# Scores of the latent attention heads as three f16 products of scaled high and low parts, in place of f32 products

## What is computed

```python
h = rms_norm(x, g_norm) * (1 + scale[:, None, :]) + shift[:, None, :]
proj = h @ w_in      # split: q_lat, kv_lat, k_rope, z_a, q_b, k_b, v_b, z_b
qa = (rms_norm(q_lat, g_qa) @ w_uq)    # 8 heads of 96, the last 32 rotated
kv = (rms_norm(kv_lat, g_kva) @ w_ukv) # k_nope (64) and va (64) of each head
ka = concat(k_nope, rotate(k_rope))    # the rotary part is shared by the heads
oa = softmax(qa @ ka.T * MLA_SCALE) @ va
ob = softmax(qb @ kb.T * GQA_SCALE) @ vb
x = x + gate * (concat(oa * silu(z_a), ob * silu(z_b)) @ w_out)
```

## Time and profile before

| | |
|---|---|
| median of 3 runs | 2541.19 us (2537.12 to 2541.44) |
| the profiled execution | 2537.28 us, its span 2535.5 us |
| PE busy | 2341.6 us, 92% of the span |
| DVE busy | 1371.3 us, 54% |
| ACT busy | 974.1 us, 38% |
| POOL busy | 790.5 us, 31% |
| mean granted TensorE clock | 0.977 |
| HBM traffic | 128.07 MB, 51 GB/s over the span |

### The profile page before, as it was taken

How to read it: one execution, slowest core, us unless ns; L and a number is a source line. 1 busy time by engine, 2 the same in 40 slices (tenths; PEclk the granted TensorE clock), 3 DMA queues, 4 the chain that set the end, 5 groups by cost and what they waited for, 6 DMA issues and landing times.

```text
span 2535.5 us, 44397 instructions
## 1 busy us (share of the span) xinstructions
PE 2341.6 (92%) x16106; PEld 1392.5 (55%) x16106; DVE 1371.3 (54%) x2444; ACT 974.1 (38%) x2202; POOL 790.5 (31%) x1325
## 2 busy tenths in 40 slices
PE   3888998899999999999989899889999999999997
PEld 1445544456556656656545455445556666665654
DVE  3645454566555555556535444446566555555563
ACT  0233333225444444444422333422354444444442
POOL 0553221664222122123036432146533113212210
PEclk7999999999999999999999999999999999999999
DMA  8712112120000000000412000132000000000001
GB/s 285 253 42 67 50 67 86 50 100 10 18 17 8 25 17 18 16 17 17 165 59 92 18 26 8 42 110 108 9 11 25 17 33 25 8 33 25 0 26 42
DMA packets 63236, 129.43 MB, mean 51 GB/s; under 512 B 6690, under 2 KB 31368, under 8 KB 63132
## 3 DMA queue, kind: packets, MB, share of 16 engines
q1 hardware_dynamic: 63136, 128.09, 14.5%
HBM read 115.44 MB, written 12.63 MB: 51 GB/s over the span
## 4 chain that ended last, share of the span: by engine, by line
PE 72%; DVE 16%; issue 5%; ACT 2%; POOL 2%; DMA 2%; SPq 1%; DVEq 0%; POOLq 0%; ACTq 0%
PE psum L600 55%; PE psum L590 10%; PE psum L808 6%; DVE region L1071 3%; DVE nmax L1054 3%; DVE hT L910 3%; ACT region L1225 1%; POOL region L1279 1%; DVE region L1029 1%; DVE KTa L872 1%; DMA Wout<-in_w_ada 1%; DVE region L1080 1%; PE psum L610 1%; PE psum L594 0%; DVE region L1031 0%
## 5 line engine op out<-in xcount | busy, mean ns | idle before, releaser
L1225 ACT ACTIVATE region<-psum 128x512 f16<-128x512 f32 x640 | 353.5, 594 | 758.5 <-PE psum L590 758.3
L600 PE MATMUL psum<-Wq,hT 128*128 128x512 f32 (+1 forms) x1536 | 611.1, 544 | 6.6 <-DVE KTa L872 5.0
L1071 DVE TENSOR_TENSOR region<-psum,region 128x512 f16<-128x512 f32 x640 | 415.7, 683 | 293.4 <-ACT region L1225 292.7
L590 PE MATMUL psum<-ident,region 128*128 128x128 f32 (+1 forms) x3208 | 436.9, 277 | 25.6 <-DVE Va L966 10.5
L600 PEld LDWEIGHTS psum<-Wq,hT 128*128 128x128 f32 x1536 | 285.0, 191 | 251.2 <-issue 224.9
L1054 DVE TENSOR_REDUCE nmax<-psum 128x1 f32<-128x1024 f32 (+1 forms) x384 | 398.7, 1038 | 40.0 <-PE psum L600 39.0
L590 PEld LDWEIGHTS psum<-ident,region 128*128 128x128 f32 (+1 forms) x3208 | 356.4, 140 | 109.7 <-issue 78.4
L600 PE MATMUL psum<-Wout,region 128*128 128x512 f32 x768 | 354.3, 606 | 9.2 <-DVE region L1039 6.8
L600 PE MATMUL psum<-KTa,region 96*128 96x512 f32 x640 | 312.9, 604 | 18.6 <-DVE region L1029 12.9
L1279 POOL TENSOR_TENSOR region<-region,rope_sb 128x64 f32<-128x64 f32 (+3 forms) x384 | 158.3, 434 | 332.5 <-DVE region L1025 316.1
L1217 ACT ACTIVATE region<-psum,nmax,unscale 128x1024 f32<-128x1024 f32 (+1 forms) x192 | 204.4, 1065 | 142.1 <-DVE nmax L1057 141.6
(11 more groups left out here) (110 smaller groups left out, 2107.8 us busy)
## 6 DMA issues: line engine op xcount, KB each, us to landing
Wout<-in_w_out SPq DMA_DIRECT2D x8, 2048.0 KB, 9.4
Va<-in_w_ada SPq DMA_DIRECT2D x12, 1024.0 KB, 5.4
Wq<-in_w_in SPq DMA_DIRECT2D x6, 2048.0 KB, 15.2
xn<-x_after_layer SPq DMA_DIRECT2D x24, 512.0 KB, 3.3
xn<-in_x_sample SPq DMA_DIRECT2D x16, 512.0 KB, 3.2
Wq<-in_w_ada SPq DMA_DIRECT2D x3, 2048.0 KB, 13.1
Wout<-in_w_ada SPq DMA_DIRECT2D x3, 2048.0 KB, 13.6
x_after_layer<-region SPq DMA_DIRECT2D x12, 512.0 KB, 2.6
```

Source lines behind the costliest of these rows:

```text
L590: return nc.tensor.transpose(out, in_, ident[0:n, 0:n])
L600: last = nc.tensor.matmul(out, lhsTs[k], rhss[k], start=k == 0, stop=k == n - 1)
L1071: nc.vector.tensor_tensor(PT[:, 1, pt_block(h, S, 4 * c):pt_block(h, S, 4 * c) + 4, :], psum[:, T_BANK + b, :].rearrange("p (c n) -> p c n ...
L1225: nc.scalar.activation(PT[:, 0, pt_block(h, S, 4 * c):pt_block(h, S, 4 * c) + 4, :], psum[:, T_BANK + b, :].rearrange("p (c n) -> p c n", ...
```

## The change

Latent keys and queries are scaled by powers of two and split into a high and a low f16 part as DVE takes them out of PSUM (`split` in place of a copy, for `k_a^T` and `q_a^T`). A score is then the sum of three f16 products: high by high, low query by high key, high query by low key. The row maximum of a latent head is multiplied by the factor that undoes the scaling, as for grouped heads, and the exponential takes the same factor as its scale. The scaling needs bounds on keys and queries: four more strided pieces of weights, and `w_uq` of both layers, are loaded at the start and reduced by DVE. `Wuq` of layer 0 is loaded there, and no longer between the first key steps. `KTa` and `QTa` keep their size. The rows of the second layer's modulation, which lie in `KTa`, are rearranged to keep to a free half of it.

```diff
-        KTa = sb("KTa", [QK, HEADS, SMAX])
+        KTa = sb("KTa", [QK, 2, HEADS, SMAX], F16)
...
-                    if part == 1:
+                    if part == 1 and l:
                         sp.dma_start(Wuq[:, :, :], w_uq[l].rearrange("(k p) n -> p k n", p=P)).then_inc(s["wuq_loaded"], 16)
...
                 sp.dma_start(up_v[:, l, :, :], w[:, :, 1, :]).then_inc(s["v_weights_loaded"], 16)
+                sp.dma_start(up_k[:, l, :, :], w[:, :, 0, :]).then_inc(s["v_weights_loaded"], 16)
                 w = w_in[l].rearrange("(k p) n -> p k n", p=P)
                 sp.dma_start(in_v[:, l, :, :], w[:, :, C_ZB - KVH * GD:C_ZB]).then_inc(s["v_weights_loaded"], 16)
+                sp.dma_start(in_rope[:, l, :, :], w[:, :, C_ZA - ROPE:C_ZA]).then_inc(s["v_weights_loaded"], 16)
+            sp.dma_start(Wuq[:, :, :], w_uq[0].rearrange("(k p) n -> p k n", p=P)).then_inc(s["wuq_loaded"], 16)
+            sp.dma_start(up_q1, w_uq[1].rearrange("(k p) n -> p k n", p=P)).then_inc(s["v_weights_loaded"], 16)
...
                         if h < HEADS:
-                            last = product(out[:, keys], [QTa[0:QK, h, :]], [KTa[:, h, keys]])
+                            last = product(out[:, keys], [QTa[0:QK, a, h, :] for a in (0, 1, 0)],
+                                           [KTa[:, a, h, keys] for a in (0, 0, 1)])
...
-            dve.wait_ge(s["v_weights_loaded"], 16 * 2 * DEPTH)
+            dve.wait_ge(s["v_weights_loaded"], 16 * (4 * DEPTH + 1))
+            dve.wait_ge(s["wuq_loaded"], 16)
             nc.vector.tensor_reduce(rinv[:, 0, 4:6], up_v, AX_XY, ALU.max, apply_absolute_value=True)
+            nc.vector.tensor_reduce(rinv[:, 0, 6:8], up_k, AX_XY, ALU.max, apply_absolute_value=True)
+            nc.vector.tensor_reduce(rinv[:, 2, 0:2], Wuq[:, :, :], AX_X, ALU.max, apply_absolute_value=True)
+            nc.vector.tensor_reduce(rinv[:, 2, 2:4], up_q1, AX_X, ALU.max, apply_absolute_value=True)
+            nc.vector.tensor_reduce(maxima[:, 6:8], in_rope, AX_XY, ALU.max, apply_absolute_value=True)
...
                         elif name in ("k_a^T0", "k_a^T1"):
-                            last = nc.vector.tensor_copy(KTa[:, 4 * c:4 * c + 4, tokens(t)],
-                                                         ps[0:QK, :].rearrange("p (h n) -> p h n", h=4))
+                            last = split(KTa[:, 0, 4 * c:4 * c + 4, tokens(t)], KTa[:, 1, 4 * c:4 * c + 4, tokens(t)],
+                                         ps[0:QK, :].rearrange("p (h n) -> p h n", h=4), a_scale[0:QK, l, r:r + 1])
...
                     elif name in ("q_a^T0", "q_a^T1"):
-                        last = nc.vector.tensor_copy(QTa[0:QK, 4 * c:4 * c + 4, :], blocks[0:QK])
+                        last = split(QTa[0:QK, 0, 4 * c:4 * c + 4, :], QTa[0:QK, 1, 4 * c:4 * c + 4, :], blocks[0:QK],
+                                     a_scale[0:QK, l, 2:3])
...
                     last = nc.vector.reduce_max(nmax[:, h:h + 1], scores_buf(h, S), AX_X, negate=True)
-                    if h >= HEADS:
-                        then(last)
-                        last = nc.vector.tensor_scalar(nmax[:, h:h + 1], nmax[:, h:h + 1], unscale[:, l:l + 1], None, ALU.mult)
+                    then(last)
+                    back = unscale[:, l:l + 1] if h >= HEADS else a_unscale[:, l, r:r + 1]
+                    last = nc.vector.tensor_scalar(nmax[:, h:h + 1], nmax[:, h:h + 1], back, None, ALU.mult)
...
-                    scale = 1.0 if h < HEADS else unscale[:, l:l + 1]
+                    scale = a_unscale[:, l, r:r + 1] if h < HEADS else unscale[:, l:l + 1]
```

More of the change, by code:

```diff
@@ L183, in encoder @@
         cT = sb("cT", [P, KD, 2])
-        maxima = sb("maxima", [P, 4 * DEPTH])
+        maxima = sb("maxima", [P, 7 * DEPTH])
         rows1_sb = sb("rows1_sb", [32, P])
@@ L218, in encoder @@
         rtmp = rtmp.rearrange("p (a n) -> p a n", a=2)
-        QTa = part(region1, HEADS * P).rearrange("p (h n) -> p h n", h=HEADS)
+        QTa = part(region1, HEADS * P).bitcast(F16).rearrange("p (a h n) -> p a h n", a=2, h=HEADS)
         region2 = sb("region2", [P, 5 * D + MIX])
@@ L251, in encoder @@
         in_v = v_weights[:, DEPTH * MIX:DEPTH * (MIX + KD * KVH * GD)].rearrange("p (l k n) -> p l k n", l=DEPTH, k=KD)
+        up_k = v_weights[:, DEPTH * (MIX + KD * KVH * GD):DEPTH * (2 * MIX + KD * KVH * GD)] \
+            .rearrange("p (l h d) -> p l h d", l=DEPTH, h=HEADS)
+        in_rope = Vb[:, :, :, :].rearrange("p c a n -> p (c a n)").bitcast(F32)[:, 0:DEPTH * KD * ROPE] \
+            .rearrange("p (l k n) -> p l k n", l=DEPTH, k=KD)
+        up_q1 = KTb[:, :, :, :].rearrange("p a g n -> p (a g n)").bitcast(F32)[:, 0:QR // P * HEADS * QK] \
+            .rearrange("p (k n) -> p k n", k=QR // P)
         ADA_N = 512
@@ L448, in ada1_bias @@
                 for r in range(2):
-                    sp.dma_start(mod1_rows[r:r + 1, 0:ADA1_TILES, :],
-                                 b_ada[1:2, 0:2 * D].rearrange("o (h n) -> o h n", n=2 * ADA1_N)).then_inc(s["bias1_loaded"], 16)
-                    sp.dma_start(mod1_rows[r:r + 1, ADA1_TILES:2 * ADA1_TILES, 0:ADA1_N],
+                    for a in range(2):
+                        sp.dma_start(mod1_rows[r:r + 1, a, 0:ADA1_TILES, :],
+                                     b_ada[1:2, 0:2 * D].rearrange("o (h a n) -> o a h n", a=2, n=ADA1_N)[:, a]) \
+                            .then_inc(s["bias1_loaded"], 16)
+                    sp.dma_start(mod1_rows[r:r + 1, 0, ADA1_TILES:2 * ADA1_TILES, :],
                                  b_ada[1:2, 2 * D:3 * D].rearrange("o (h n) -> o h n", n=ADA1_N)).then_inc(s["bias1_loaded"], 16)
@@ L561, in _ @@
                     sp.wait_ge(s["mm_free"], rounds.now())
-                    sp.dma_start(mod[2:4, 0:2 * D].rearrange("r (h n) -> r h n", n=2 * ADA1_N),
-                                 mod1_rows[:, 0:ADA1_TILES, :]).then_inc(s["mod_stored"], 16)
+                    for a in range(2):
+                        sp.dma_start(mod[2:4, 0:2 * D].rearrange("r (h a n) -> r a h n", a=2, n=ADA1_N)[:, a],
+                                     mod1_rows[:, a, 0:ADA1_TILES, :]).then_inc(s["mod_stored"], 16)
                     sp.dma_start(mod[2:4, 2 * D:3 * D].rearrange("r (h n) -> r h n", n=ADA1_N),
-                                 mod1_rows[:, ADA1_TILES:2 * ADA1_TILES, 0:ADA1_N]).then_inc(s["mod_stored"], 16)
+                                 mod1_rows[:, 0, ADA1_TILES:2 * ADA1_TILES, :]).then_inc(s["mod_stored"], 16)
                 if q + 1 < len(inst):
@@ L576, in _ @@
                 if q == 0:
-                    sp.wait_ge(s["mod_stored"], 48)
+                    sp.wait_ge(s["mod_stored"], 64)
                     for r1 in range(2):
@@ L893, in modulation_columns @@
                 dve.wait_ge(s["cols_ready"], l + 1)
-                top = maxima[:, 6 * l:6 * l + 2]
+                top = maxima[:, 12 * l:12 * l + 2]
                 nc.vector.tensor_reduce(top, gs[:, 2 * l:2 * l + 2, :], AX_X, ALU.max, apply_absolute_value=True)
@@ L952, in value_scales @@
                                             float(KVR), 1e-30, ALU.mult, ALU.max)
-                    then(nc.vector.tensor_scalar(v_bound[:, both, 1], maxima[:, 6 * l:6 * l + 2],
+                    then(nc.vector.tensor_scalar(v_bound[:, both, 1], maxima[:, 12 * l:12 * l + 2],
                                                  maxima[:, 4 + l:5 + l], float(D), ALU.mult, ALU.mult))
-                    then(nc.vector.tensor_scalar(v_bound[:, both, 1], v_bound[:, both, 1], 1e-30, None, ALU.max))
+                    nc.vector.tensor_scalar(a_bound[:, l, 0:2], maxima[:, 12 * l:12 * l + 2],
+                                            maxima[:, 6 + l:7 + l], 2.0 * D, ALU.mult, ALU.mult)
+                    nc.vector.tensor_scalar(a_bound[:, l, 2:3], maxima[:, 10 + l:11 + l],
+                                            2.0 * QR * MLA_SCALE, 1e-12, ALU.mult, ALU.max)
+                    then(nc.vector.tensor_scalar(a_unscale[:, l, :], maxima[:, 8 + l:9 + l].broadcast_to([P, 2]),
+                                                 float(KVR), 1e-12, ALU.mult, ALU.max))
+                    nc.vector.tensor_tensor(a_bound[:, l, 0:2], a_bound[:, l, 0:2], a_unscale[:, l, :], ALU.max)
+                    then(nc.vector.tensor_scalar(v_bound[:, both, 1], v_bound[:, both, 1], 1e-30, None, ALU.max))
+                    then(nc.vector.tensor_scalar(a_bound[:, l, :].bitcast(U32), a_bound[:, l, :].bitcast(U32),
+                                                 0x7F800000, None, ALU.bitwise_and))
+                    nc.vector.tensor_scalar(a_unscale[:, l, :], a_bound[:, l, 0:2], a_bound[:, l, 2:3], 2.0 ** -28,
+                                            ALU.mult, ALU.mult)
+                    then(nc.vector.reciprocal(a_scale[:, l, :], a_bound[:, l, :]))
+                    nc.vector.tensor_scalar(a_scale[:, l, :], a_scale[:, l, :], 2.0 ** 14, None, ALU.mult)
```

23 lines of the change are left out of this document (16 added, 7 removed).

## The result

The changed kernel takes 2616.7 us (median of 4 runs, 2615.19 to 2618.09), the kernel before 2539.15 us on the same chip: 77.5 us slower, ratio 1.0305 with a 95% interval of 1.0288 to 1.0321. Forecast were 2602 us, 2555 to 2640. The profiled execution took 2617.5 us with a span of 2615.7.

The account below looks back on a forecast made before the run. PE sets the time on average, but waits for DVE where the change touches, and SP's queue bounds the start. Terms 12 + 13 + 19.5 + 3 + 11 + 2 + 3 = 63.5 us on 2537.3 gave 2601, stated as 2602; range 2555 to 2640.

Parts of the forecast that it names:

- PE's gain for a block: Scores on PE: a block of 512 keys gets 0.215 us cheaper, at most 68.8 us for 320 blocks.
- Split 1.44 us and factor 0.23: DVE: a split holds it 1.44 us, 0.84 more than a copy (bounds 0.60 and 1.0); each row maximum 0.23 more.
- Steady tiles: Query tiles waiting for DVE: 1.2 us longer each at S 1024, 2.5 at S 512; tile terms +12 and +13.
- The waits of the drains: Three PE waits for DVE per drain, each behind two more splits, 1.68 us; four drains at 4.9, +19.5.
- The start: Added loads ahead of SP's modulation store shift every later step: +10.4 us, plus 0.6 for DVE's reductions; bounds 6 and 16.
- The scales of q2: Ten small DVE instructions of about 0.2 us ahead of `h^T` in q2: +2 us.
- The clock: Low PE clock after drain waits: two more stretches of 1.6 us lost, +3; bounds 0 and 13.
- The gain of the first tiles: First query tile of an instance, no late DVE behind it: gains 2.4 us at S 1024, 0.9 at S 512.
- the first (2480): Rival: PE bounds everywhere and DVE's work is hidden, so all 68.8 us come: 2480 us; chance 0.03.
- the second one of 50: Rival: tiles gain 45 us at S 1024, some 5 at S 512; the rest loses 35: 2522 us; chance 0.05.
- The third: Rival: start and drains cost half, the tiles nothing: about 2555 us down to no change; chance 0.05.
- The fourth: Rival: new short waits in the tiles lower the clock too, adding 77 us: about 2675; chance 0.05.

Follow-up runs that it names:

- e12: Changed kernel with keys and queries copied once to f16, three products on high halves, no low parts, scales, factor or start loads: 2513.7 us.
- e1: Changed kernel keeping only its start loads, reductions and scale instructions, with f32 scores, plain copies and no factor: 2551.1 us.
- e9: Changed kernel with products that nobody reads (2, 4 and 4) filling PE's three waits of each drain: 2599.8 us.
- e11: Kernel before the change with products that nobody reads (none, 2 and 2) in PE's three waits of each drain: 2535.5 us.
- e2: Changed kernel without the factor on the row maximum of latent heads, the exponential taking scale 1.0: 2584.9 us.

## Why the prediction was right, and where it was not

- **PE's gain for a block: right.** 0.215 us for each f16 product in the steady tile; scores 246.8 us of busy time, forecast some 240. That most of it would not reach the end was right too; in e12 28 us do.
- **Split 1.44 us and factor 0.23: right** to the hundredth in the timeline of DVE. Neither bound was needed.
- **Steady tiles: right.** +0.95 us at S 1024 in layer 0 and +1.08 in layer 1, forecast 1.2; +2.5 at S 512 in q2 (72.09 to 74.60), forecast 2.5. The chain that gave it, `out1`, `y_a^T` and `q_b^T0` each later by what DVE needs, stands in the rows with waits of 0.91, 0.75 and 0.45. The passage into the second tile at S 512 was cheaper than forecast; that is the row with 5.5 for 10. In q0 this is luck: the passage had a granted clock of 0.95 before and 1.00 in the change.
- **The waits of the drains: right.** The second went from 1.97 to 3.65 us, the third from 1.90 to 3.58, 1.68 each as forecast. The first was not "about 2": it went from 0.77 to 2.65 in q1, so its growth came too, from a smaller size.
- **The start: right in size**, 9.7 measured in e1 for 11. The path was half wrong: the modulation came 6.6 us later and not 10, and x the rest.
- **The scales of q2:** the wait ahead of `h^T` grew from 4.1 to 5.2 us, 1.1 for 2. `value_scales` got eight small instructions there, where the section on the change says nine and the forecast counted ten.
- **The clock: the term that was mis-sized.** I took two more low stretches, +3, "bounds 0 and 13". e9 and e11 give 10 to 13, at or near the upper bound. The row I went by was one stretch of four microseconds behind one wait; what I did not count is that the third wait of a drain does it too, as the rows of q1 show (4.14 us for the first scores, 2.75 in e9), and that the first tile runs at the low clock for a while too.
- **The gain of the first tiles: did not come.** "The first tile has no late DVE behind it, and gains 2.4 in its slots 0 to 11" is the step that failed; with 0.9 at S 512 that is 6.6 us. With the clock about as before (e9) those stretches still cost 9.0, which is the third wait (6.7) and a little more. The factor is a good part of the reason: without it (e2) they are 6.4 us shorter than in the change, of which the slightly higher clock gives at most 3.8. I had charged it to slots of the steady tiles and not to the first. e12 can't decide it, since its clock there is lower than before. That error and the clock's, 14 to 17 us, are partly offset by the cheaper tiles at S 512.
- **The ends of the range.** The bounds named for them give 2578 (for 2575) and 2617 (for 2625: 2602 with 5 more for the start and 10 for the clock). Both lie well inside 2555 to 2640.

Of the rivals, the first (2480) needed a gain of 68.8 and the second one of 50; e12 leaves both no ground, even with the 9.5 us. The third had the tiles at nothing; those of S 1024 cost 12.3 us. The fourth placed the low clock in the steady tiles: there it stayed at 1.00, as the rows said; it fell in the first tiles.

The Trainium skill, Perfetto Trace Analysis, Identifying the Most-Contended Engine, says to optimize the engine of highest occupancy first, though for TensorE it judges the headroom by other measures than busy time. PE was that engine at 92%, and e12 made it cheaper at no cost to others: 28 us of 68.8. In the kernel before, the engine with 54% already decided many slots. The next section of that page of the Trainium skill, Optimization Strategy, says to look up what blocks each gap; that is what told it here.
